# Forget-gate attention: turning the weights by a product with a diagonal matrix, and masks that open the score blocks

## The reference

```python
for start in range(0, s, Q_BLOCK):          # Q_BLOCK = 128
    end = start + Q_BLOCK
    logits = jnp.einsum('bhqd,bhkd->bhqk', qh[:, :, start:end], kh[:, :, :end]) * scale
    logits = logits + cum[:, :, start:end, None] - cum[:, :, None, :end]
    causal = (start + jnp.arange(Q_BLOCK))[:, None] >= jnp.arange(end)[None, :]
    p = jax.nn.softmax(jnp.where(causal, logits, -jnp.inf), axis=-1)
    outs.append(jnp.einsum('bhqk,bhkd->bhqd', p.astype(vh.dtype), vh[:, :, :end]))
```

## Time and profile before

| | |
|---|---|
| time, median of 3 runs | 1571.34 us (1571.28 to 1571.98) |
| the profiled execution | 1572.2 us |
| its span in the profile | 1570.4 us |
| TensorE busy | 1530.0 us, 97% of the span |
| VectorE, ScalarE busy | 806.9 us, 613.3 us |
| attention stage | about 313 to 392 us of the span |
| TensorE, VectorE, ScalarE busy within 350 to 358 us | 7.42, 6.45, 5.79 us |

### The profile page before, as it was taken

How to read it: one execution, slowest core, us unless ns; L and a number is a source line. 1 busy time by engine, 2 the same in 40 slices (tenths; PEclk the granted TensorE clock), 3 DMA queues, 4 the chain that set the end, 5 groups by cost and what they waited for, 6 DMA issues and landing times.

```text
span 1570.4 us, 21288 instructions
## 1 busy us (share of the span) xinstructions
PE 1530.0 (97%) x7585; PEld 1115.6 (71%) x7585; DVE 806.9 (51%) x1492; ACT 613.3 (39%) x1180; POOL 139.8 (9%) x160
## 2 busy tenths in 40 slices
PE   8999999999999999999999999999998999999969
PEld 6787788856788888888888888877886333333347
DVE  4868765687335666655234346764556222222256
ACT  5656633476324545554224322555246100000033
POOL 1015200010000000000000001100001122222110
PEclk9999999999999999999999999999999999999989
DMA  5333243210333333333333321322254999999541
GB/s 209 114 103 101 81 121 95 80 61 28 99 90 93 95 96 98 94 100 94 98 97 97 98 81 56 120 67 81 81 179 159 409 411 410 408 397 381 218 180 54
DMA packets 93570, 232.96 MB, mean 148 GB/s; under 512 B 15664, under 2 KB 16176, under 8 KB 89264
## 3 DMA queue, kind: packets, MB, share of 16 engines
q1 hardware_dynamic: 80032, 209.75, 38.7%
q0 software_dynamic: 13168, 21.87, 4.3%
q10 hardware_dynamic: 288, 0.23, 0.0%
HBM read 282.05 MB, written 16.84 MB: 190 GB/s over the span
## 4 chain that ended last, share of the span: by engine, by line
PE 88%; DVE 7%; ACT 2%; DMA 2%; issue 1%; POOL 0%; SPq 0%; ACTq 0%; DVEq 0%; POOLq 0%
PE ps L350 21%; PE ps L352 21%; PE ps L351 21%; PE ps L1098 10%; PE ps L1117 5%; PE ps L1077 1%; DVE acc L2175 1%; PE ps L1821 1%; DVE Pb L2417 1%; DVE lo L345 1%; PE ps L1807 1%; PE ps L1689 1%; PE ps L1833 1%; ACT Pb L2064 1%; DVE Pb L2428 1%
## 5 line engine op out<-in xcount | busy, mean ns | idle before, releaser
L345 DVE TENSOR_TENSOR lo<-raw,hi 128x512 fp32r<-128x512 f32 x288 | 198.3, 710 | 289.2 <-ACT hi L335 289.0
L335 ACT ACTIVATE hi<-raw 128x512 fp32r<-128x512 f32 x288 | 176.3, 632 | 381.1 <-PE ps L352 380.7
L350 PE MATMUL ps<-HTh,lo 128*128 128x512 f32 x688 | 269.9, 392 | 5.7 <-DVE HTl L442 3.6
L352 PE MATMUL ps<-HTh,hi 128*128 128x512 f32 x688 | 267.8, 389 | 0.0
L351 PE MATMUL ps<-HTl,hi 128*128 128x512 f32 x688 | 267.8, 389 | 0.0
L350 PEld LDWEIGHTS ps<-HTh,lo 128*128 128x128 f32 x688 | 129.1, 188 | 35.7 <-issue 3.6
L352 PEld LDWEIGHTS ps<-HTh,hi 128*128 128x128 f32 x688 | 129.2, 188 | 27.1
L351 PEld LDWEIGHTS ps<-HTl,hi 128*128 128x128 f32 x688 | 129.2, 188 | 26.1
L350 PE MATMUL ps<-hi,HTl 128*128 128x512 f32 (+1 forms) x352 | 137.4, 390 | 0.5 <-ACT zs L1934 0.4
L352 PE MATMUL ps<-hi,HTh 128*128 128x512 f32 (+1 forms) x352 | 133.9, 380 | 0.0
L351 PE MATMUL ps<-lo,HTh 128*128 128x512 f32 (+1 forms) x352 | 133.7, 380 | 0.0
(11 more groups left out here) (400 smaller groups left out, 2517.3 us busy)
## 6 DMA issues: line engine op xcount, KB each, us to landing
raw<-in_wstream SPq DMA_DIRECT2D x384, 256.0 KB, 2.6
slot<-in_wexp SPq DMA_DIRECT2D x64, 1024.0 KB, 18.3
slot<-in_wexp SPq DMA_DIRECT2D x16, 2048.0 KB, 22.2
cum<-cum_d POOLq DMA_DIRECT2D x16, 256.0 KB, 3.9
fcb<-fc_d POOLq DMA_DIRECT2D x16, 256.0 KB, 3.7
YG<-ye_d SPq DMA_DIRECT2D x3, 1024.0 KB, 10.1
X<-in_x SPq DMA_DIRECT2D x4, 512.0 KB, 5.7
xg_d<-xn POOLq DMA_DIRECT2D x4, 512.0 KB, 4.2
```

The lines of the kernel that those rows point to most:

```text
L335: act.activation(hi[:, i % RING, :], raw[:, i % RING, :], ACT.Copy).then_inc(hi_ready, 1)
L345: dve.tensor_tensor(lo[:, i % RING, :], raw[:, i % RING, :], hi[:, i % RING, :].bitcast(F32), ALU.subtract).then_inc(lo_ready, 1)
L350: pe.matmul(o, al, bh, start=start, stop=False)
L352: return pe.matmul(o, ah, bh, start=False, stop=stop)
```

## The change

`turned` no longer transposes scaled weights by the identity. `normalize` builds a diagonal matrix `Dg` for each query block from the reciprocals of the row sums, and `turned` multiplies the unscaled weights by it, which transposes and scales them in one product. `Dg` holds the matrices of two heads, so `normalize(h)` waits until the turns of head h - 2 are done. The causal mask products move into a function of their own, `masks(p, g)`, which opens the accumulation of each score block; the score products follow and close it. The waits at the head of `scores` move into `masks`. At the start all three groups of masks go ahead of the scores, and for later pairs the masks of groups 0 and 1 go together.

```diff
+        Dg = at("Dg", [P, 2, T, P], F32, A + 91)
...
-            def scores(p, g):
+            def masks(p, g):
                 bank, parts = fox_bank(p, g), FG[g][1]
                 if p == 0 and g == 0:
                     pe.wait_ge(mats_loaded, 48)
...
                 for i, o in parts:
                     n = (i + 1) * P
                     for e in range(2):
+                        pe.matmul(ps[:, bank + e, o + n - P:o + n], identb[:, :], maskL[:, :], start=(i, o) == parts[0],
+                                  stop=False, skip_group_check=True)
+
+            def scores(p, g):
+                bank, parts = fox_bank(p, g), FG[g][1]
+                for i, o in parts:
+                    n = (i + 1) * P
+                    for e in range(2):
                         r = slice(HD * e, HD * e + HD)
-                        pe.matmul(ps[:, bank + e, o:o + n], qT[r, p, i * P:(i + 1) * P], kT[r, p, 0:n], start=True, stop=False)
-                    for e in range(2):
-                        mm = pe.matmul(ps[:, bank + e, o + n - P:o + n], identb[:, :], maskL[:, :], start=False, stop=True)
+                        mm = pe.matmul(ps[:, bank + e, o:o + n], qT[r, p, i * P:(i + 1) * P], kT[r, p, 0:n], start=False,
+                                       stop=(i, o) == parts[-1], skip_group_check=True)
                         if (i, o) == parts[-1]:
                             mm.then_inc(fx_qk, 1)
...
-                        tr = pe.transpose(ps[:, bank, o + (i - j) * P:o + (i - j + 1) * P],
-                                          Pb[h % 4][:, FOFF[i] + j * P:FOFF[i] + (j + 1) * P], ident[:, :])
+                        tr = pe.matmul(ps[:, bank, o + (i - j) * P:o + (i - j + 1) * P],
+                                       Pb[h % 4][:, FOFF[i] + j * P:FOFF[i] + (j + 1) * P], Dg[:, h % 2, i, :],
+                                       start=True, stop=True)
...
             for g in range(NG_):
+                masks(0, g)
+            for g in range(NG_):
                 scores(0, g)
             for p in range(H1 // 2):
                 if p + 1 < H1 // 2:
+                    masks(p + 1, 0)
+                    masks(p + 1, 1)
                     scores(p + 1, 0)
                     scores(p + 1, 1)
...
                 if p + 1 < H1 // 2:
+                    masks(p + 1, 2)
                     scores(p + 1, 2)
...
                 ch.link(dve.reciprocal(fst[:, 2, k_, :], fst[:, 1, k_, :]))
-                for i in range(T):
-                    pb = Pb[k_][:, FOFF[i]:FOFF[i] + (i + 1) * P]
-                    ins = dve.tensor_scalar(pb, pb, fst[:, 2, k_, i:i + 1], None, ALU.mult)
-                ins.then_inc(fx_pn, 1)
+                if h >= 2:
+                    dve.wait_ge(fx_t, h - 1)
+                dve.tensor_tensor(Dg[:, h % 2, :, :], ident[:, :].unsqueeze(1).broadcast_to([P, T, P]),
+                                  fst[:, 2, k_, :].unsqueeze(2).broadcast_to([P, T, P]), ALU.mult).then_inc(fx_pn, 1)
```

## The result

| | before | after |
|---|---|---|
| time, median | 1571.66 us (4 runs) | 1585.24 us (4 runs) |
| ratio | | 1.0084, 95% interval 1.0067 to 1.0102 |
| profiled execution, span | 1572.2, 1570.4 us | 1583.54, 1581.5 us |
| VectorE busy, TensorE busy | 806.9, 1530.0 us | 798.6, 1541.8 us |

What follows compares the result with a forecast made beforehand. The prediction took TensorE, busy for 97% of the span, to bound the kernel. Product 17.1, VectorE -2.4, masks -2.6 and start +0.6 gave +12.7 us, so 1584.0 us, range 1580.0 to 1589.0.

Steps and rivals of the forecast that it cites:

- The product's price: In `turned`, 160 float32 products at 0.223 us replace transposes at about 0.11 us: 17.1 us more, bounds 16.2 to 18.8.
- the rival of 1620 us: In `turned`, a product costs four transposes, as the skill's rule says: +48 us, 1620 us; 2 in 100.
- VectorE's relief: `normalize` gets about 0.58 us shorter a head, so TensorE's waits ahead of second turns shrink: 2.4 us recovered, or zero.
- Masks first: Batched masks and adjoining score parts make TensorE switch kinds less often: 2.6 us saved, bounds 0 and 4.0.
- The two joins: Score parts following each other, twice a pair, save 0 to 2.7 us over 14 joins; half, 1.3 us, was taken.
- The start: At the stage's start, masks ahead of all scores delay the first turn by 0.2 us: +0.6 us, 0.5 either way.
- The wait that stays: Ahead of the second turn, TensorE still waits for ScalarE's copies, 0.16 us in each of seven pairs.
- The sum: All terms for the attention stage together: +12.7 us, giving 1584.0 us.
- That a product runs at a transpose's rate: In `turned`, products cost 0.11 us as transposes do, so the kernel gets 4.4 us faster, 1566.9 us; 2 in 100.
- The rival in which the wait moves to ScalarE and stays as long: Ahead of turns, ScalarE's copies come late, so 1.8 us are not recovered: 1585.8 us; 10 in 100.
- the rival of dearer changeovers and joins that give nothing: On TensorE, changeovers cost more and joins save nothing: +15 to +20 us, 1586 to 1591 us; 8 in 100.

Runs made afterwards that it cites:

- e1: The changed kernel with the masks back behind each score part, so only the turn by a product stays; 1587.69 us, ratio 1.0099 to the kernel before.
- e3: The changed kernel with turns made transposes by the identity again, `Dg` built but unread, result left unscaled; 1566.45 us, ratio 0.9958 to the kernel before.
- e8: The changed kernel with the turn's product in fp32r and the masks behind the score parts; 1571.09 us, ratio 0.9991 to the kernel before.
- e4: The changed kernel with each mask pair directly ahead of its own score part, not batched; 1587.96 us, ratio 1.0098 to the kernel before.
- e6: The changed kernel with exponentials and `Dg` written as fp32r, so the turn is an fp32r product; 1567.21 us, ratio 0.9964 to the kernel before.
- e2: The changed kernel with turns as transposes of weights scaled by VectorE again, so only the masks change stays; 1572.29 us, ratio 1.0000 to the kernel before.
- e5: e2 with VectorE's copy for a pair's first turn moved ahead of the logits of group 1; 1571.32 us, ratio 0.9994 to the kernel before.

## Why the prediction was right, point by point

- **The product's price** was put at 17.1 us (16.2 to 18.8). The trace has 320 records, as foreseen, and a turn takes twice what it took. L562 in the second block had shown the right cost of an operation that the stage did not contain. The size came out at the high end: with the masks left behind, the turns of e1 take 18.8 us more than those of the kernel before, summed from start to start and without waits. A turn ahead of scores takes 2.39 to 2.43 us there, 0.16 to 0.20 above twenty records at 0.1117, where I had allowed 0.07. A slip stands in the same sum: three turns, not two, go ahead of `out0` (the second of pair 6 as well), which moves it by 0.1 us. By the rule of the Trainium skill ("TensorE: Matmul & The Clock Gate", Terms), four to one, this term would have been 53 us; the runs show a turn of 2.31 to 2.34 us (changed kernel) against 1.12 to 1.15 (e3), two to one, and the rival of 1620 us is out.
- **VectorE's relief** was put at 2.4 us of waits, and e1 shows 2.3: TensorE's waits inside the stage were 2.9 us ahead of the second turns and 0.56 ahead of group 0 of pair 2, and in e1 seven waits of 0.16 us are left. The parts were right too: 692 ns an operation, 0.5 us idle ahead of all sixteen and so no wait on `fx_t` to speak of, no wait of TensorE for VectorE's copy after. The longer turns do a part of this: with short fp32r turns (e8) a wait of 0.54 us for the logits of pair 1 stays.
- **Masks first** was mis-sized, and it is the largest error. I booked 2.6 us less 0.6 at the start, and they give 4.3 (e1 against after), beyond my upper bound of 4.0 less 0.1. Six masks take 0.42 us (0.45 expected), so that term holds. The two joins save 2.36 - 1.93 = 0.43 us a pair, all of the 0.19 us a part that I had halved. What I did not book is that a turn ahead of a mask is 0.09 us shorter than ahead of a score, 1.2 us over the stage, of which the wait for ScalarE's copies takes back 0.7. e4 shows that most of what pays is going between masks and scores less often. From the rule that a change of tiling mode drains the engine ("TensorEngine Tiling (Array Packing)", Key Properties, of the Trainium skill) I had worked out that the joins would save all of it, and here they do; but no run separates the tiling mode from the data type, which changes at the same place.
- **The start** was put at +0.6 us: 0.2 late, and the saving booked for the first of the seven pairs lost. The first turn starts 8.50 us after the first piece, against 8.47 before, so the booked saving (0.63 us by the rows) is lost and nothing more: the stall is there (1.09 us, ended by VectorE at 317.14), and shorter scores make up for it. With the saving at its real size the term is 0.7.
- **The wait that stays**, ScalarE's copies, is there seven times, at 0.26 us rather than 0.16. ScalarE's first copy starts 0.20 us behind the piece that follows the turn (the mask at 333.90, the copy at 334.10), where it was 0.11 us behind a score product: the mask starts 0.1 us sooner after the turn, and that much more is waited for.
- **The sum** was +12.7 us, in the stage +12.14. I had booked 1.7 us too little for the price and 2.3 us too little for what the masks give net of the start, and the two nearly cancelled: the account of the mechanism was right, and that the sum came out within 0.6 us of the stage is in part luck. The time rose by 13.6 us; the 1.4 us between stage and time are within the interval, and no run traces them (the two profiled executions are 11.1 us apart in their spans).
- **The rivals.** That a product runs at a transpose's rate falls for float32 and holds for fp32r (e6), which I had not priced. The rival in which the wait moves to ScalarE and stays as long falls: 1.8 us are left of 2.9. It holds in part, since only 1.1 of these were booked. In the rival of dearer changeovers and joins that give nothing, the first half came true (e1) and the second did not. The profile also puts 1.0 us of idle weight loading down to `Dg`, but no matmul waits for it, and `values` ahead of those turns takes 2.30 us as before.

What the prediction did not see is how the edits hang together. I took each for a sum of its own, which held since they were made together. The masks alone give nothing (e2), since VectorE is late by as much as TensorE gains; it takes the lighter VectorE for them to pay.

## What to carry to other kernels

Before folding a scaling into a transpose, count the records: in float32 a product left two where the transpose left one, and 160 of them cost about 18 us of the stage on the engine that sets the time, to take 8 us from one that does not. Price an operation that a stage lacks from another stage that has it at the same shape. When one engine waits a little for another in every turn of a loop (0.3 to 0.7 us here), an edit to the waiting one alone can show nothing (e2, e5), and the worth of a pair of edits has to be tried as a pair.

## What the runs showed of the hardware

A 128x128 product of 128 columns in fp32r took 0.12 us (e6, ten in 1.18 us from start to start, changeover included), nearly what a float32 transpose takes (e3, ten in 1.15 us), and half of a float32 product (20 records in 2.34 us in the changed kernel). I had not expected 128 columns in fp32r to be no faster than the transpose. Masks in bf16 over all rows between float32 score parts over half of the rows cost (2.97 - 2.35) / 2 = 0.31 us for each time that the kind changes and changes back (e4 against the changed kernel, which has two such changes a pair fewer). A turn took 2.43 us ahead of a score part and 2.33 us ahead of a mask (e1, e4).
